# The up product of the dense layers as seven block products, with weight sums made by accumulating loads

## What is computed

```python
def sqrelu_mlp(h, w1, w2):                 # after each mixer, D=1024, F=4096
    u = jax.nn.relu(jnp.einsum('bsd,df->bsf', h, w1))
    return jnp.einsum('bsf,fd->bsd', u * u, w2)

for i in range(2):
    hn = rmsnorm(h, norm_mix[i])
    h = h + (conformer_conv(hn, ...) if i % 2 == 0 else pool_mixer(hn, ...))
    h = h + sqrelu_mlp(rmsnorm(h, norm_mlp[i]), mlp_w1[i], mlp_w2[i])
return rmsnorm(h, final_norm)
```

## Time and profile before

| | |
|---|---|
| median of 3 runs | 886.61 us (886.11 to 886.99) |
| profiled execution, span from first to last instruction | 884.7 us |
| PE busy in it | 874.4 us (99%) |
| PE weight loads busy | 740.7 us (84%) |
| DVE busy | 700.1 us (79%) |
| ACT busy | 464.1 us (52%) |
| POOL busy | 140.0 us (16%) |
| DMA, mean over the span | 110 GB/s, 97.62 MB |
| chain that ended last | PE 95%, DVE 2%, DMA 1%, ACT 1% |

### The profile page before, as it was taken

How to read it: one execution, slowest core, us unless ns; L and a number is a source line. 1 busy time by engine, 2 the same in 40 slices (tenths; PEclk the granted TensorE clock), 3 DMA queues, 4 the chain that set the end, 5 groups by cost and what they waited for, 6 DMA issues and landing times.

```text
span 884.7 us, 11889 instructions
## 1 busy us (share of the span) xinstructions
PE 874.4 (99%) x4383; PEld 740.7 (84%) x4383; DVE 700.1 (79%) x946; ACT 464.1 (52%) x675; POOL 140.0 (16%) x122
## 2 busy tenths in 40 slices
PE   8999999999999999999999999999999999999997
PEld 8888887899888888888888889988888888888886
DVE  6899999768786968776778788897786968776866
ACT  6898976247272544536273544637272544536243
POOL 1699970560000020000000040000000000000000
PEclk9999999999999999999999999999999999999999
DMA  9766732305413142331314222122313142331202
GB/s 302 198 166 150 188 73 98 143 1 191 143 47 143 57 175 77 118 133 57 142 48 167 77 73 90 48 98 94 142 47 142 52 174 77 125 127 64 72 1 95
DMA packets 49255, 97.62 MB, mean 110 GB/s; under 512 B 1562, under 2 KB 18978, under 8 KB 48324
## 3 DMA queue, kind: packets, MB, share of 16 engines
q1 hardware_dynamic: 48068, 89.54, 29.4%
q0 software_dynamic: 1008, 7.34, 4.0%
q10 hardware_dynamic: 144, 0.26, 0.1%
HBM read 87.70 MB, written 2.10 MB: 101 GB/s over the span
## 4 chain that ended last, share of the span: by engine, by line
PE 95%; DVE 2%; DMA 1%; ACT 1%; issue 0%; SPq 0%; DVEq 0%; ACTq 0%
PE ps L1454 19%; PE ps L1452 19%; PE ps L1453 19%; PE ps L1717 10%; PE ps L1715 10%; PE ps L1716 10%; PE ps L1530 3%; PE ps L1471 1%; PE ps L1629 1%; PE ps L1634 1%; PE ps L1630 1%; DMA h<-in_x 1%; DVE tok L894 0%; DVE act_lo L900 0%; DVE tok L928 0%
## 5 line engine op out<-in xcount | busy, mean ns | idle before, releaser
L1452 PE MATMUL ps<-act_hi,w_hi 128*128 128x512 f32 (+1 forms) x688 | 254.9, 370 | 0.0
L1453 PE MATMUL ps<-act_lo,w_hi 128*128 128x512 f32 (+1 forms) x688 | 254.2, 369 | 0.0
L1454 PE MATMUL ps<-act_hi,w_lo 128*128 128x512 f32 (+1 forms) x688 | 254.2, 369 | 0.0
L1715 PE MATMUL ps<-w_hi,u_hi 128*128 128x512 f32 x392 | 152.7, 390 | 0.0
L1717 PE MATMUL ps<-w_hi,u_lo 128*128 128x512 f32 x392 | 152.7, 390 | 0.0
L1716 PE MATMUL ps<-w_lo,u_hi 128*128 128x512 f32 x392 | 152.5, 389 | 0.0
L685 ACT ACTIVATE relu<-ps 128x512 f32<-128x512 f32 x36 | 21.5, 597 | 242.8 <-PE ps L1454 242.8
L1452 PEld LDWEIGHTS ps<-act_hi,w_hi 128*128 128x128 f32 x688 | 129.7, 188 | 21.8
L1454 PEld LDWEIGHTS ps<-act_hi,w_lo 128*128 128x128 f32 x688 | 129.6, 188 | 21.8
L1453 PEld LDWEIGHTS ps<-act_lo,w_hi 128*128 128x128 f32 x688 | 129.7, 188 | 21.7
L1172 DVE TENSOR_TENSOR w_lo<-w_raw,w_hi 128x1024 fp32r<-128x1024 f32 x70 | 85.1, 1220 | 58.0 <-ACT w_hi L706 58.0
(11 more groups left out here) (237 smaller groups left out, 1264.0 us busy)
## 6 DMA issues: line engine op xcount, KB each, us to landing
w_raw<-in_mlp_w SPq DMA_DIRECT2D x32, 1024.0 KB, 5.0
w_raw<-in_mlp_w SPq DMA_DIRECT2D x16, 2048.0 KB, 8.0
w_raw<-in_conv_w SPq DMA_DIRECT2D x16, 512.0 KB, 5.5
prod_a<-prod_a POOLq DMA_DIRECT2D x7, 1024.0 KB, 7.9
w_raw<-in_conv_w SPq DMA_DIRECT2D x2, 2048.0 KB, 11.0
h<-in_x SPq DMA_DIRECT2D x4, 512.0 KB, 5.8
out<-tok SPq DMA_DIRECT2D x7, 256.0 KB, 2.0
gain<-in_norm_mlp SPq DMA_DIRECT2D x2, 512.0 KB
```

The source lines that it names most:

```text
L1452: nc.tensor.matmul(dst, lh, rh, start=(n == 0), stop=False)
L1453: nc.tensor.matmul(dst, lh, rl, start=False, stop=False)
L1454: return nc.tensor.matmul(dst, ll, rh, start=False, stop=(n == count - 1))
L1715: nc.tensor.matmul(dst, lh, rh, start=(f == 0 and (opens or i not in (0, 5))), stop=False)
```

## The change

The up product of groups 1 to 7 of both layers becomes seven block products too.

- **PE.** Each product is 2 feature tiles x 4 chunks x 3 = 24 matmuls of 256 columns (`bank_quarter`), 168 in a group in place of 96 of 512 columns. Their results lie in banks 2, 3, 0, 1, 0, 1, 2.
- **Weight sums.** The blocks of w1 and w2 are loaded as 512 KB quarters, each sum by a plain load from SP and further loads of the same place from POOL with `accum_op=ALU.add`. For a group, w1 takes 5 plain and 4 accumulating loads, w2 likewise. One place (`w_chain`) passes through four stages S1, S2, S4 by one accumulation each, every one waiting until the stage before has been split; `b_chain` likewise (T1, T2, T4). DVE's sums of w2 are gone.
- **Activation sums.** In group 0 of each layer DVE makes the four sums of the activations once (`x_block`, `x_step`: eight operations of 128x1024) and ACT and DVE split them (`x_hi`, `x_low`).
- **Results.** DVE combines the seven products to the four quarters of u by seven operations of 128x512 (`sum_two` to `sum_21`), one ACT copy stands ahead of them, and relu and square then work on SBUF.
- **Adds.** The ten additions of 128x512 become five of 128x1024 (`add`), by other signs in acc; `acc_out` becomes four operations of 128x1024 at the very end of `mlp_up_last`.
- **Orders.** SP, POOL, ACT and DVE get new hand-written orders. The low part of the pooling weights moves from DVE to POOL, behind `acc_out`. The pooling weights and the pooling scale are loaded late in layer 0.

The core of the diff:

```diff
@@ SP, ahead of layer 0
             sp.wait_ge(c2_lo_ok, 4)
-            for k in range(2):
-                load_m2(0, 0, k)
+            load_first_b(0)
             sp.wait_ge(y_ok, 1)
             sp.dma_start(b2, row(conv_b2[0])).then_inc(b2_in, 16)
             sp.wait_ge(c2b_lo_ok, 4)
             load_m1(0, 0)
+            sp.wait_ge(band_ok, 1)
+            load_b(0, 0, b_chain, 0, 1, b_chain_in)
             sp.wait_ge(y_ok, NB)
             sp.dma_start(gain[:, 0, :], row(norm_mlp[0])).then_inc(gain_in[0], 16)
+            load_groups(0)
             sp.dma_start(gain[:, 1, :], row(pool_scale[0])).then_inc(gain_in[1], 16)
-            sp.wait_ge(turned, 4 * GEN_MLP0 + NB)
+            sp.wait_ge(up_mm, first_part(0, MIDDLE) + 3)
             sp.dma_start(pw_raw, ...).then_inc(pw_in, 16)
-            load_groups(0)
@@ SP, one group
+                def period(w, opens=False, closes=False):
+                    if not closes:
+                        sp.wait_ge(w2_lo_ok, 7 * w + (splits + 1))
+                        load_b(layer, w + 1, b11, 0, 0, b11_in)
+                        sp.wait_ge(w2_lo_ok, 7 * w + (splits + 2))
+                        load_b(layer, w + 1, b_t3, 0, 1, b_t3_in)
+                    if not opens:
+                        sp.wait_ge(w1_lo_ok, first_part(layer, w) + W_AT[4])
+                        load_w(layer, w + 1, w_s3, 0, 0, w_s3_in)
+                        sp.wait_ge(w1_lo_ok, first_part(layer, w) + W_AT[5])
+                        load_w(layer, w + 1, w_chain, 1, 0, w_chain_in)
+                        sp.wait_ge(w1_lo_ok, first_part(layer, w) + W_AT[6])
+                        load_w(layer, w + 1, w_a22, 1, 1, w_a22_in)
...
@@ POOL, one group
+                def period(w, closes=False):
+                    add_t2(layer, w)
+                    if not closes:
+                        add_t3(layer, w + 1)
+                    add_s3(layer, w + 1)
+                    add_s1(layer, w + 1)
+                    add_t4(layer, w)
+                    add_s2(layer, w + 1)
+                    add_s4(layer, w + 1)
+                    if not closes:
+                        add_t1(layer, w + 1)
@@ DVE, mlp_up_last, its last line
+                acc_out(layer)
@@ DVE, group 0 of a layer
                 if first:
                     dve.wait_ge(acc_zero, layer + 1)
-                    upper_sums()
                     b_low(0)
                     b_low(1)
                     b_low(2)
-                    first_diff()
+                    dve.wait_ge(act_lo_ok, 4 * (GEN_MLP0, GEN_MLP1)[layer] + NB)
+                    x_block(layer, 1, z1, 1, 1)
+                    x_block(layer, 2, z3, 0, 1)
+                    x_step(layer, 3, z3, z1, z3, ALU.subtract)
+                    x_block(layer, 4, z2, 0, 0)
+                    x_step(layer, 5, z2, z3, z2, ALU.add)
+                    x_step(layer, 6, z1, z1, z2, ALU.subtract)
+                    third_sum(n + 2)
                     a_low(0)
-                    last_sum()
                     a_low(1)
+                    first_sum()
+                    second_sum()
                     b_low(3)
-                    w1_low(n + 4, 0)
+                    a_low(2)
+                    a_low(3)
+                    w_low(layer, 1, 3)
+                    w_low(layer, 1, 0)
+                    w_low(layer, 1, 1)
...
+                fourth_sum()
+                b_low(4)
+                add(1, 0, acc[:, 1])
                 a_low(4)
+                add(2, 2, acc[:, 0])
+                b_low(5)
                 a_low(5)
                 b_low(6)
                 a_low(6)
+                add(4, 4, h[:, 0:2, 0:512])
                 if first:
+                    x_low(layer, 0)
+                    dve.wait_ge(up_mm, LAYER_PARTS * layer + GF)
+                    x_block(layer, 7, z4, 1, 0)
+                    x_step(layer, 8, z4, z4, z2, ALU.subtract)
+                    x_low(layer, 1)
+                w_low(layer, w + 1, 2)
+                add(5, 6, h[:, 2:4, 0:512])
+                add(6, 8, h[:, 0:2, 512:D])
+                if first:
+                    x_low(layer, 2)
+                    x_low(layer, 3)
@@ PE, mlp_up
-                for j in range(GF):
-                    n = 4 * w + (4 * GROUPS * layer + j)
-                    pe.wait_ge(w1_lo_ok, n + 1)
-                    pe.wait_ge(m_added, 10 * w + (LAYER_ADDS * layer - 3 + j))
-                    for c in range(NC):
-                        last = product(ps[:, UP_BANK[j], :], (m1_hi[:, j, c, :], m1_lo[:, j, c, :]),
-                                       act_tile(c, slice(0, S)), c, NC)
+                right = ((0, 0), 0, 1, (1, 0), 2, (1, 1), 3)
+                for i, bank in enumerate((2, 3, 0, 1, 0, 1, 2)):
+                    pe.wait_ge(w1_lo_ok, n + W_AT[i])
+                    if i < 4:
+                        pe.wait_ge(m_added, 5 * w + (LAYER_ADDS * layer - 1 + i // 2))
+                    if i == 4:
+                        pe.wait_ge(up_sum_ok, summed + 1)
+                    if i == 5:
+                        pe.wait_ge(up_sum_ok, summed + 3)
...
+                            nc.tensor.matmul(dst, lh, rh[:, c], start=(c == 0), stop=False)
+                            nc.tensor.matmul(dst, lh, rl[:, c], start=False, stop=False)
+                            last = nc.tensor.matmul(dst, ll, rh[:, c], start=False,
+                                                    stop=(c == 3))
```

631 lines of the change are left out of this document (434 added, 197 removed).

## The result

The changed kernel takes **999.4 us** (median of 4 runs, 996.5 to 1001.1) against 886.7 us of the kernel before in 4 runs beside it: a ratio of **1.127, 95% interval 1.125 to 1.129**. The prediction said 906 us with a range of 886 to 940. The direction was right; the size was not: 113 us more instead of 19.

What follows compares the result with a forecast made beforehand. PE (TensorE) was taken as the bound: its matmul count times their spacing. From a span of 884.7, -22.8 + 4 + 17.5 + 4 + 12.6 + 4.1 gave 904.1, plus 1.9 made 906 us; range 886 to 940.

Steps and rivals of the forecast that it cites:

- TensorE's gain: Dense-layer groups: half-width matmuls save 1.63 us a group, leaving 39.2 us; -22.8 us for 14 groups.
- DVE and ACT at nothing in a group: In a group DVE needs 32.4 us, under 39.2, and ACT stays near 60%; costed at nothing.
- The loads: Weight loads in groups: w_chain's chain takes 34 to 41 us against 39.2; 0.3 us a group, +4 us for 12.
- Rival 1: Accumulation chain late before down product 4: 12 groups each wait 1 to 4 us, total 914 to 950; chance 25%.
- The price of a transfer: DMA engine time per quarter in a group: plain 1.3 to 1.5 us, accumulating 2.4 or 2.75 us.
- one sixth more: Accumulating quarters: if shorter rows cost them the same sixth as plain loads, 2.75 us instead of 2.4.
- It fits, barely: A group's transfers hold the DMA engines 32 us at best, 37 us at worst, of 39.2 us.
- The gain behind band_ok: Start of dense layers: the norm gain's load waits on SP for band_ok, lands at 192.9; PE waits, +17.5 us.
- Clock: After PE idles, the slower clock costs 2.0 us after the long wait and half that per opening; +4 us.
- Openings: Each layer's opening: PE waits 6.3 us for DVE, at down product 4, then before group 1; +12.6 us for two.
- End of layer 0: acc_out moves ahead of layer 1's w1_low on DVE, delaying PE's turn; +4.1 us, POOL's pooling low part costing nothing.

Runs made afterwards that it cites:

- e3: The changed kernel with each accumulating load replaced by a two-column POOL memset, so no second loads and no weight sums: 914.6 us, ratio 1.031.
- e10: e3 with the gain's load ahead of the band_ok wait on SP and the pooling weights' low part back on VectorE: 891.9 us, ratio 1.0063.
- e2: The changed kernel with every accumulating load made a plain load of the same 512 KB, so weight sums are left out: 914.8 us, ratio 1.032.
- e12_more_room: e6 with descriptor room for POOL's queue at its default instead of 4096 bytes: four accumulating w1 quarters took 14.7 us instead of 18.8.
- e4: The changed kernel with S1's cast moved behind b_high(4) and a_high(4) on ACT, its low part behind a_low(4) on DVE: 970.3 us.
- e5: e4 with T1's cast and low part also moved behind part 5 of the up product, cutting the load loop: 967.7 us, ratio 1.091.
- e11_no_x_sums: e10 with activation sums, and the casts and low parts concerned, cut to two columns in layer 1 alone: 886.7 us, ratio 1.0004.
- e7_pool_sums: e5 with every accumulating load replaced by a POOL addition in SBUF, and the plain loads of w_s3 and b_t3 dropped: 1055.8 us, ratio 1.191.
- e6: A separate kernel of 512 KB loads only, plain and accumulating, alone and together: four accumulating w1 quarters took 0.74 of 19.1 us, four plain 1.7 us each.

## Why the prediction was right or wrong

**TensorE's gain: right.** 39.2 us a group was said; 39.11 stands in the groups that nothing holds up (all of e3's and e10's, nine of e2's ten).

**DVE and ACT at nothing in a group: right**, 33.9 us against my 32.4. In e2 and e3 no group past the opening waits for them.

**The loads: wrong, and this is the step that failed.** The prediction put the chain of `w_chain` at "34 to 41 us against 39.2" and priced it at 0.3 us a group, "+4 us", "since the parts rarely all coincide". It came out at 48.3 us in the group shown above, and the ten groups take 47.3 on average: 8.1 us over 39.2 in each, where 0.3 was said. Two things in it were wrong.

First, the landings. 3.7 and 5.5 us were right for transfers alone (3.8, 5.8 and 6.2). In the changed kernel their medians are 5.0 and 7.4 us plain, 8.8 and 9.1 accumulating, and the plain load in the loop above took 10.65. With loads that do not add (e2), still 18 in 39.1 us, they are 4.0 to 6.2, and the loop closes in time. So the adding is the cause of the 8 us, and it works through the landings. Second, the way round. The loop also passes T1 and POOL's queue, which I had not followed. Rival 1 had the mechanism and the place; its "1 to 4 us" was 8, so its 914 to 950 was too low as well.

The price of a transfer was too low too, but less than it looks. "A plain quarter holds the DMA engines 1.3 to 1.5 us, an accumulating one 2.4 us, or 2.75" came from GB/s in windows with the share above 1.00. In packet time the measured prices are 1.7 and 3.1 to 3.5 us; the row of 346 GB/s stands at a share of 1.15, which is 1.7 us of packet time too. As rates the prediction's figures nearly hold: 1.4 us and 2.7 us in e12_more_room. The row for accumulating was one of 1 MB from SBUF to SBUF, 8 KB in one piece in each partition, where a quarter of w1 comes from HBM in rows of 1 KB; that the guess of one sixth more for it came out near the mark was luck. "It fits, barely" may well be true of the rates (36 to 40 us, an estimate). The mistake was to read from it that nearly nothing is lost, when every load also waits for others in a closed loop.

e4 and e5 split the 8 us: about 3 are order and loop, which reordering gave back, about 5 remained. What holds these 5 stays open: the loops of landings at a mean share of 0.94 to 0.99, the engines' limit, or both. Whether a better order could bring the groups nearer to 39.1 was not tried.

**The gain behind band_ok: right.** Said: landing at 192.9, +17.5. It landed at 185.71 + 5.47 = 191.2, DVE waited 17.0 and TensorE 15.5 (bounds 14 and 21); the start is 18.7 us later, most of the rest being clock (0.78 from 192 to 205), and moving the load gave 17.8 us at this place and 14.7 in the end. I said `band_ok` at 187.2 by POOL quickening while DVE is held; 185.3.

**Clock: the mechanism right, the size too small.** I gave 1.0 for an opening. In layer 1's opening of e10_free_sums TensorE waits 5.1 us until 605.57; the granted clock falls to 0.50 within this wait and returns at about 610.5:

```profile
606.00:610.00 4.00, 4.00 (x20) 4.00 (x20) 4.00 (x5) 0.67 (x1) 0.00 (x0) 0.50 0.00 0
610.00:614.00 4.00, 4.00 (x33) 4.00 (x33) 2.70 (x4) 2.65 (x4) 0.00 (x0) 0.93 0.55 166
```

Half of 4.0 us, 0.07 of 4, and 0.2 from 605.57 to 606 are 2.5 us of lost clock. e11_no_x_sums bears it out: there the clock stays at 1.00, the two waits are 3.7 us shorter, and the opening is 6.2 us shorter, 3.7 + 2.5. The two waits, the clock and the gain of 1.75 a group give 6.8 + 2.5 - 1.75 = 7.6 us of the 8.5 measured; the 0.9 left I have not traced, it is there in e11 too.

**Openings: right in mechanism and nearly in size.** 6.3 us of waiting was said, 6.8 found, in the order said; e11 shows that DVE's list is the cause. Together with the clock an opening costs 8.0 to 8.9 us more than before (e3, e10), where 5.7 was said.

**End of layer 0: a term was missing.** +2.8 was said for the stage, +14.8 found. "POOL's new low part of the pooling weights ends before DVE asks" was true (531.7, asked for at 540) and beside the point: while POOL reads two operands, DVE's four splits take 11.2 us instead of 4.6 (in e3 above, and from 571.14 in the changed kernel). Undoing it gave 5.3 us. The Trainium skill ("SBUF — State Buffer", Who interferes with whom) states that a VectorE instruction with two SBUF inputs contends with a GpSimd instruction that reads SBUF; both this row and e7_pool_sums agree. I had used that very rule for `band_ok`, where it helped the change, and not looked for it where a step was moved onto POOL. The 7.8 us that e10 still has between the layers (acc_out, the low part on DVE, the clock behind a wait of 5.0 us) I have not taken apart further.

**The total if the weight sums were free.** TensorE gains 24 us in 14 groups; openings and layer end give back over 30. e10_free_sums says so: with openings and layer end as they are, the change would not have won even with weight sums at no cost.

## What to carry to other kernels

This change traded matmuls for sums and paid on other engines. For such a one, add up the DMA engines' time for a group with prices of the same kind of transfer (adding on arrival, length of rows, from HBM), and if no row of the trace has that kind, time it first, alone and in company; one small kernel would have given both here. When the total comes near the time it has to hide in, do not read it as hidden: the slowest medians of the landings grew here from 3.8 to 7.4 us plain and from 6.2 to 9.1 accumulating, and every closed loop of load, split and reload has to be followed round, through the queues of all engines that it passes. Of each step that is moved to another engine, ask both whether it is in time and whom it slows while it runs.

## What the runs showed of the hardware

- An accumulating load takes about twice the DMA engines' time of a plain one of the same bytes: 3.1 to 3.5 us of packet time against 1.7 for 512 KB (e6, e12), and the same one at a time. Alone it lands 2.0 to 2.4 us later (5.8 and 6.2 against 3.8, the plain ones issued by SP). POOL's instruction for it takes 1.2 to 1.4 us in e6, a plain one 0.71 to 0.77 in e2.
- The DMA share is no scale that ends at 1.00: it read 1.22 over 10 us with four accumulating quarters under way (192 GB/s) and 1.10 with four plain ones (365 GB/s).
- The same 18 transfers at 241 GB/s without adding left TensorE without a gap in the groups; with adding, the groups of the changed kernel moved 195 GB/s and took 8 us longer. GB/s alone says little about whether traffic fits.
- With 4096 bytes of room for POOL's descriptors the fourth accumulating quarter in 1-KB rows waits for room, 8.6 us with no other loads and 13.4 us beside plain ones; with the default it does not.
- Two-operand work on POOL in SBUF beside DVE's splits: four of them in 11.2 us instead of 4.6 where POOL is busy almost without pause, 7.3 us more on DVE for 21 us of POOL in a group of e7_pool_sums.
- A stop of 6.2 us of TensorE in the groups (385.0 to 391.2) was followed by some 4.5 us of work at the 1.2 GHz level; windows of 2 us from 388 read 0.71, 0.50, 0.50, 0.58 and 1.00. The loop that sets the pace in that group has no piece of TensorE in it.
